# A compression MLP's input kept in token order: contiguous evictions, matmul operand read at a step of eight

## The reference, cut to what matters

```python
CMP_BLOCK = 32; CMP_STRIDE = 16; CMP_HIDDEN = 256; HEAD_DIM = 64

def compress(kf, pos_emb, w1, w2):
    B, Tp, G, D = kf.shape
    c = kf.reshape(B, Tp // CMP_STRIDE, CMP_STRIDE, G, D)
    blocks = jnp.concatenate([c[:, :-1], c[:, 1:]], axis=2) + pos_emb[:, None, :]
    nc = blocks.shape[1]
    flat = jnp.moveaxis(blocks, 3, 2).reshape(B, nc, G, CMP_BLOCK * D)
    return jax.nn.silu(flat @ w1) @ w2

kc = compress(nsa_pad[:, :, 0], cmp_pos[0], cmp_w1[0], cmp_w2[0])
vc = compress(nsa_pad[:, :, 1], cmp_pos[1], cmp_w1[1], cmp_w2[1])
```

## Time and profile before

| | us |
|---|---|
| median of 3 runs (lowest, highest) | 3833.23 (3830.82, 3834.14) |
| the profiled execution's own time | 3834.14 |
| its span | 3832.3 |
| the stage `tables` in it, from its first DMA issue to the last copy | 1995.2 to 2103.7 |
| the matmuls of line 2335 in it | 2052.8 to 2097.1 |

### The profile page before, as it was taken

The page is one execution under the profiler, slowest core; times in us unless marked ns, Lnnn a source line. Parts: engine busy times, 40 slices in busy tenths (PEclk is TensorE's granted clock), DMA queues, the critical chain, the costliest instruction groups (busy, mean ns, idle before and its releaser), DMA issues. The chain is left out here.

```text
span 3832.3 us, 47790 instructions
## 1 busy us (share of the span) xinstructions
PE 3473.3 (91%) x20510; PEld 3240.4 (85%) x20510; DVE 1363.3 (36%) x1984; ACT 611.1 (16%) x1124; POOL 1201.0 (31%) x571
## 2 busy tenths in 40 slices
PE   6989888999999999989897787997777999999998
PEld 6989767889999999978784675886557999999998
DVE  4951145524323232430011545555114432323242
ACT  4310133221000000110001332332111100000012
POOL 4433112633444444423120211111002344444442
PEclk8999876899999999989998896998557999999999
DMA  4111221221111111222312321001112111111111
GB/s 126 45 34 52 82 25 47 60 97 39 45 44 45 44 45 44 62 99 93 100 28 59 83 51 33 7 7 38 51 51 86 34 48 41 47 42 46 43 46 63
DMA packets 302537, 204.14 MB, mean 53 GB/s; under 512 B 61633, under 2 KB 283155, under 8 KB 301784
## 3 DMA queue, kind: packets, MB, share of 16 engines
q1 hardware_dynamic: 296800, 200.65, 18.4%
q10 hardware_dynamic: 5528, 0.45, 0.1%
HBM read 158.87 MB, written 33.40 MB: 50 GB/s over the span
## 5 line engine op out<-in xcount | busy, mean ns | idle before, releaser
L236 PE MATMUL ps<-u_r,wslots_r 128*128 128x364 f32 x4608 | 772.1, 330 | 0.0
L236 PEld LDWEIGHTS ps<-u_r,wslots_r 128*128 128x128 f32 x4608 | 770.6, 189 | 0.0
L203 POOL TENSOR_TENSOR wslots_r<-rawm,sb_ones 128x1024 fp32r<-128x1024 f32 x133 | 322.1, 2422 | 908.9 <-PE ps L236 873.2
L236 PE MATMUL ps<-hn_r,wslots_r 128*128 128x364 f32 x2880 | 589.1, 330 | 13.2 <-POOLq L197 13.2
L236 PE MATMUL ps<-low_r,wslots_r 128*128 128x364 f32 x2688 | 543.3, 330 | 16.7 <-POOLq L197 15.0
L236 PEld LDWEIGHTS ps<-hn_r,wslots_r 128*128 128x128 f32 x2880 | 496.8, 189 | 13.7 <-POOLq L197 13.7
L236 PEld LDWEIGHTS ps<-low_r,wslots_r 128*128 128x128 f32 x2688 | 461.5, 189 | 17.1 <-POOLq L197 15.1
L205 POOL TENSOR_TENSOR wslots_r<-rawm,wslots_r 128x1024 fp32r<-128x1024 f32 x133 | 379.9, 2857 | 10.4
L1878 DVE TENSOR_TENSOR xT<-xT,ps 128x1092 f32<-128x1092 f32 x80 | 103.3, 1292 | 650.6 <-PE ps L236 650.6
L1600 PE MATMUL ps<-hn_r,wslots_r 128*128 128x364 f32 x1392 | 279.1, 334 | 17.7 <-POOLq L1570 9.1
L1600 PEld LDWEIGHTS ps<-hn_r,wslots_r 128*128 128x128 f32 x1392 | 240.7, 191 | 24.2 <-DVE Z L1830 10.0
(11 more groups left out here) (594 smaller groups left out, 4858.0 us busy)
## 6 DMA issues: line engine op xcount, KB each, us to landing
rawm<-in_w_down SPq DMA_DIRECT2D x64, 512.0 KB
rawm<-in_w_up SPq DMA_DIRECT2D x63, 512.0 KB
raw<-in_w_in_even SPq DMA_DIRECT2D x28, 512.0 KB
xT<-x_saved SPq DMA_DIRECT2D x2, 4368.0 KB
xT<-in_cache_fox_kv SPq DMA_DIRECT2D x16, 512.0 KB
more_r<-more_r SPq DMA_DIRECT2D x28, 256.0 KB
panel_raw<-in_w_in_odd SPq DMA_DIRECT2D x6, 1024.0 KB
x_saved<-Z SPq DMA_DIRECT2D x1, 4368.0 KB
```

What stands on the lines that cost most here:

```text
L203: nc.gpsimd.tensor_tensor(r32(half[0][:, g % 2]), raw[:, g % 2], one, ALU.mult).then_inc(s["high"], 1)
L236: mm = pe.matmul(view[n % 2][:, c, :], r32(half[a][:, n % 2, k, :]), r32(t["x"][b][:, k, CH * c:CH * (c + 1)]), start=(k == 0 and (a, b) = ...
```

## The change

`X[kv]` becomes flat, in token order: unit `n` and pair `a` lie at element `8 n + a`. The eviction of line 2383 then writes contiguous runs (two of 128 elements for the prompt, one of 256 for the sample). The matmul reads its 385 columns at a step of 8 elements, which is 32 bytes. The sixteen rows of the position embedding land in the last 16 elements, which are the same two columns as before, by one DMA for each `kv` instead of two, and the count that PE waits for falls from 8 transfers to 6.

```diff
-    X = [arena([P, 8, UNITS + 2]) for _ in range(2)]
+    X = [arena([P, 8 * (UNITS + 2)]) for _ in range(2)]
@@ tensor engine
-            pe.wait_ge(s["w"], 16 * 8)
+            pe.wait_ge(s["w"], 16 * 6)
@@
                 for a in range(16):
-                    mm = pe.matmul(hb, w1[:, kv, a, P * m:P * (m + 1)], X[kv][:, a % 8, a // 8:a // 8 + UNITS + 1], start=(a == 0), stop=(a == 15))
+                    c0 = 8 * (a // 8) + a % 8
+                    mm = pe.matmul(hb, w1[:, kv, a, P * m:P * (m + 1)], X[kv][:, c0:c0 + 8 * UNITS + 1:8], start=(a == 0), stop=(a == 15))
@@ scalar engine
-                for x in range(2):
-                    act.dma_start(X[kv][:, :, UNITS + x:UNITS + x + 1], I["nsa_cmp_pos"][0, kv].rearrange("(x a w o) d -> x (w d) a o", x=2, w=2, o=1)[x],
-                                  allow_slow_non_contiguous=True).then_inc(s["w"], 16)
+                act.dma_start(X[kv][:, 8 * UNITS:8 * UNITS + 16], I["nsa_cmp_pos"][0, kv].rearrange("(a w) d -> (w d) a", w=2),
+                              allow_slow_non_contiguous=True).then_inc(s["w"], 16)
@@
-                    src = bank(ps, u % 2)[:, 256 * kv:256 * kv + 256].rearrange("p (g n a) -> p g n a", g=2, a=8)
-                    n0 = 16 * u if u < 4 else 128 + 32 * (u - 4)
-                    to = X[kv][:, :, 0:128] if u < 4 else X[kv][:, :, n0:n0 + 32]
-                    dst = to.rearrange("p a (g n) -> p g n a", g=2)
+                    src = bank(ps, u % 2)[:, 256 * kv:256 * kv + 256].rearrange("p (g n) -> p g n", g=2)
                     if u < 4:
-                        dst = dst[:, :, n0:n0 + 16, :]
+                        dst = X[kv][:, 0:1024].rearrange("p (g n) -> p g n", g=2)[:, :, P * u:P * (u + 1)]
+                    else:
+                        dst = X[kv][:, 1024 + 256 * (u - 4):1024 + 256 * (u - 3)].rearrange("p (g n) -> p g n", g=2)
                     ins = A.activation(dst, src, ACT.Copy)
```

## The result

| | before | after |
|---|---|---|
| median of 4 runs, us | 3832.03 | 3875.18 |
| lowest to highest | 3826.02 to 3834.14 | 3868.13 to 3878.12 |
| the profiled execution (span), us | 3834.14 (3832.3) | 3872.16 (3870.4) |
| stage `tables` in it | 108.5 | 152.3 |
| its first matmul after the stage's start | 57.6 | 56.8 |

The ratio is 1.0115, with a 95% interval from 1.0102 to 1.0129, that is 39 to 49 us. The forecast was 3832.8; rival 1, the slow fetch, had been put at 3875 and is what came. Its exact figure is partly luck: it had +41.8 us on a kernel before at 3833.23, and what came was +43.2 on 3832.03.

The account below looks back on a forecast made before the run. PE was taken to bound the kernel (91% busy), with the stage's matmul fully on the path. Evictions -0.4, embedding 0, matmul 0 from 3834.14 gave 3833.7, or 3832.8 us on the median's scale; range 3829 to 3882.

Parts of the forecast that it names:

- rival 1: First MLP layer's matmul (line 2335): stepped fetch runs at the memory's rate, 321 to 671 ns each, about 3875 us; chance 0.34.
- What bounds the stage: Stage `tables`: the 44.28 us matmul piece is wholly on the path; SP's load issues pace the steps before it.
- Part 1: Evictions of line 2383: 271 ns less for each of 24, only the last pair on the path, -0.4 us.
- Part 2: Position embedding: two fewer DMA issues on ACT's queue, log-sigmoid up to 1.1 us earlier, covered, so 0 us.
- Part 3: Matmul of line 2335 reading its moving operand at a 32-byte step: fetch taken as free, 0 us, with little confidence.
- The bound from above: Line 2335, from ACT's stepped read: +3.0 us at most if engine peaks halve; 671 ns a MATMUL if 1.74 ns is the memory's.
- The rows: Cited for a free step: DVE's PSUM reads at step 8 (290 ns), and lines 538 and 539's 8-column products (254 ns each).

## Why the prediction was wrong, point by point

- **What bounds the stage**: right. The matmul piece is on the path in full (+44.6 in the piece, +43.8 in the stage, +43.2 in the median), and the evictions' pace is set by SP's page loads.
- **Part 1, evictions, -0.4**: right as far as the trace can tell. The eviction fell by 274 ns (271 expected) and PE's wait for ACT by 0.5. Both runs that have the cheap eviction alone stand at the kernel before, within an interval of some 4 us either way, so the 0.4 itself is not measured.
- **Part 2, embedding, 0**: right in its effect; that the log-sigmoid would start up to 1.1 us earlier was wrong, it was 0.2.
- **Part 3, the read, 0**: this is the step that failed. I took the reading that a step halves each engine's own peak, and counted PE's spare rate, 0.449 ns an element in the fp32r matmuls against 0.833 in this f32 one, as cover. By the starts that fp32r rate is 0.46 (98 MATMULs from 3001.7 to 3017.9, 364 columns each), which changes little. Half that rate, 0.92 ns a column, is even near what fp32r does at a step: 0.84 to 0.90. The fault was to carry it over from fp32r to f32, for which no row spoke. The f32 matmul took 1.80 ns a column at a step of 8, at either clock, more than twice the 0.833 that it needs in order; the runs show 1.76 to 1.80 ns a line for f32 and bf16. The prediction came near it under rival 1: the fast reads are four columns of one line, 1.8 ns for a line, and so say nothing of how fast lines can change. But that isn't the whole account either, for fp32r at steps 4 and 8 does get a line in 0.84 to 0.90 ns. Why f32 doesn't stays open.
- **The bound from above** was right to 3%: ACT's stepped read of the earlier trace rows gave 1.74 ns an element against the 1.80 measured on PE. Rival 1's +42.0 in the matmuls came out as +44.6, and its total of 3875 as 3875.18, the last digits by luck, as said under the result.
- **The rows** should have had no weight: the one reads another memory by another engine (and DVE turned out not to share the price even in SBUF), the other is too short.
- **The chances**: 0.34 for rival 1 was too low. With the only wide stepped SBUF accesses among the rows, ACT's, at half rate and near a fixed time for a line (1.74 and 1.89 ns), and a gain excluded, the slow side deserved more than half.

## What to carry to other kernels

Before a matmul's moving operand gets a step, count the 16-byte lines that it touches, and allow 1.8 ns for each: if that is more than the columns take (0.83 ns each in f32), the difference is lost on every instruction. For f32 four neighbours out of each line are free and two nearly so; where a column takes less time (0.45 ns in fp32r), two to a line already take about twice as long. For fp32r with a line for each column 0.84 to 0.90 ns was enough. Where a permutation has to be paid somewhere, pay it on the cheap side: in the few evictions (here 24 x 271 ns, mostly hidden), by the order in which PSUM is read (384 ns, free here), or on the weights if the moving side is long enough to hide them (314 ns beside 323 here), rather than in 128 matmuls that are read again and again. Price an access that the trace doesn't show by the nearest row in the same memory, even if another engine made it, as a rival of full weight, rather than by an argument on spare rate of another type. It is still a guess across engines: ACT's price happened to fit PE to 3%, DVE's would not have.

## What the runs showed of the hardware that I had not expected

- PE's price of a line is a time (about 0.69 us for 385 lines at 1.2 and at 2.4 GHz), the same to 3% for f32 and bf16, and ACT's is nearly the same, 1.82 ns, by single copies. DVE's is lower: 501 and 506 ns for 385 lines against 362 in order.
- fp32r takes 0.84 to 0.90 ns a column at steps 2, 4 and 8, and 0.45 in order: at steps 4 and 8 half the price that f32 and bf16 pay for a line, at step 2 the same.
- Two columns to a line are nearly free in f32 (339 against 323 ns) and not in fp32r (340 against 174).
- ACT reads PSUM at a step of 32 bytes at no price (384 ns against 381 to 384 in order), though it writes SBUF at a wide step at 655.
- Matmuls whose lines come slowly count as busy throughout, and in bf16 the granted clock fell to 0.50 during them without a change in the price of a line. In f32 it stayed at 1.00 (66 us in a row in the kernel after).
